# Five cross-partition totals moved inside a slab, four adaLN sums as products with ones, and second-block inputs moved later in a two-layer encoder kernel

## The reference, cut to what matters

```
shift, scale, gate = split(c @ w_ada + b)        # adaLN, once per sub-layer
u = x * (1 + scale) + shift
y = mixer(u)  or  conv_gated_mlp(u)
x = layer_norm(alpha * x + (1 + gate) * y, g, b)

mixer:  a,g,q,k,v = split(u @ w_in)
        h = silu(layer_norm(dwconv31(a * sigmoid(g))))
        o = attention(rotary(q), rotary(k), v)     # window of two 64-token chunks, with sinks
        y = concat(h, o) @ w_out
mlp:    val, gate = split(u @ w_up);  y = (val * silu(dwconv3(gate))) @ w_down
```

## Time and profile before

| what | before |
|---|---|
| time, median of 3 runs | 2124.24 us (2122.6 to 2124.82) |
| the profiled run, its span | 2124.59 us, 2122.7 us |
| TensorE busy | 2076.3 us, 98% |
| weight loads (beside the matmuls) | 1707.1 us, 80% |
| VectorE / ScalarE / GpSimd busy | 56% / 48% / 66% |
| chain that ended last | TensorE 77%, GpSimd 9%, VectorE 5%, ScalarE 4%, issue 3%, DMA 1% |
| mean granted clock of TensorE | 0.992 |
| DMA | 250 MB, mean 118 GB/s |

### The profile page before, as it was taken

One profiled execution on the slowest core, in us unless ns is written; L12 is line 12 of the kernel. 1 busy time (PEld: TensorE's weight loads), 2 busy tenths in 40 slices (PEclk: granted clock), 3 DMA queues, 4 the chain that ended last, 5 costly groups with the idle time before them and its releaser, 6 DMA issues.

```text
span 2122.7 us, 27312 instructions
## 1 busy us (share of the span) xinstructions
PE 2076.3 (98%) x9603; PEld 1707.1 (80%) x9603; DVE 1189.1 (56%) x1949; ACT 1025.4 (48%) x1830; POOL 1404.7 (66%) x1773
## 2 busy tenths in 40 slices
PE   7999999999999999999999999999999999999997
PEld 6877778787888788888788888888778888888887
DVE  5887878676514554777542545587651354332225
ACT  3574357564515665364642656235462465333332
POOL 4986767765767887875557885564546776545554
PEclk9999999999999999999999999999999999999999
DMA  8644544533434354553233333432323333434332
GB/s 296 157 131 137 159 123 137 163 109 100 123 116 124 96 159 139 155 152 99 78 100 100 113 106 92 106 96 74 95 77 104 94 96 90 124 101 123 97 92 77
DMA packets 421508, 250.06 MB, mean 118 GB/s; under 512 B 48149, under 2 KB 393085, under 8 KB 421373
## 3 DMA queue, kind: packets, MB, share of 16 engines
q1 hardware_dynamic: 420506, 248.03, 39.6%
q10 hardware_dynamic: 867, 0.29, 0.1%
HBM read 242.71 MB, written 4.26 MB: 116 GB/s over the span
## 4 chain that ended last, share of the span: by engine, by line
PE 77%; POOL 9%; DVE 5%; ACT 4%; issue 3%; DMA 1%; SPq 1%; POOLq 0%; DVEq 0%; ACTq 0%
PE fg L853 25%; PE fg L855 24%; PE fg L854 24%; POOL w_lo L1856 5%; POOL ada_acc L1927 1%; PE bank_s L939 1%; DVE bank_c L1471 1%; DMA first_ada<-in_w_ada_mix_dram 1%; ACT ada L1262 1%; POOL ssum L1983 1%; PE bank_l L865 1%; PE bank_l L876 1%; ACT w_hi L1112 1%; PE bank_t L948 0%; PE bank_t L961 0%
## 5 line engine op out<-in xcount | busy, mean ns | idle before, releaser
L1856 POOL TENSOR_TENSOR w_lo<-raw,w_hi 128x256 fp32r<-128x256 f32 (+1 forms) x1425 | 1030.1, 754 | 642.1 <-ACT w_hi L1112 641.0
L853 PE MATMUL fg<-u_hi,w_hi 128*128 128x512 f32 x2112 | 841.4, 398 | 5.3 <-POOL w_lo L1856 1.8
L855 PE MATMUL fg<-u_hi,w_lo 128*128 128x512 f32 x2112 | 826.4, 391 | 0.0
L854 PE MATMUL fg<-u_lo,w_hi 128*128 128x512 f32 x2112 | 826.2, 391 | 0.0
L1112 ACT ACTIVATE w_hi<-raw 128x1024 fp32r<-128x1024 f32 (+2 forms) x387 | 375.5, 970 | 390.2 <-PE fg L855 295.9
L853 PEld LDWEIGHTS fg<-u_hi,w_hi 128*128 128x128 f32 x2112 | 398.7, 189 | 103.0 <-issue 15.8
L855 PEld LDWEIGHTS fg<-u_hi,w_lo 128*128 128x128 f32 x2112 | 398.4, 189 | 84.7
L854 PEld LDWEIGHTS fg<-u_lo,w_hi 128*128 128x128 f32 x2112 | 398.8, 189 | 81.9 <-issue 2.9
L1471 DVE SCALAR_TENSOR_TENSOR bank_c<-glu,par,bank_c 128x512 f32<-128x512 f32 x448 | 306.2, 748 | 0.1
L1810 DVE SCALAR_TENSOR_TENSOR x<-fg,mod,x 128x512 f32<-128x512 f32 (+1 forms) x168 | 121.6, 724 | 322.6 <-PE fg L855 322.4
L855 PE MATMUL fg<-h_hi,w_lo 128*128 128x512 f32 (+1 forms) x704 | 270.1, 384 | 0.0
(11 more groups left out here) (253 smaller groups left out, 1849.4 us busy)
## 6 DMA issues: line engine op xcount, KB each, us to landing
raw<-in_w_up_dram SPq DMA_DIRECT2D x176, 512.0 KB, 3.8
ada<-in_w_ada_ffn_dram SPq DMA_DIRECT2D x48, 512.0 KB, 4.6
raw<-in_w_down_dram SPq DMA_DIRECT2D x64, 384.0 KB, 3.5
raw<-in_w_in_dram SPq DMA_DIRECT2D x40, 512.0 KB, 4.0
raw<-in_w_down_dram SPq DMA_DIRECT2D x64, 320.0 KB, 3.1
ada<-in_w_ada_mix_dram SPq DMA_DIRECT2D x32, 512.0 KB, 4.3
raw<-in_w_in_dram SPq DMA_DIRECT2D x32, 256.0 KB, 3.8
raw<-in_w_out_dram SPq DMA_DIRECT2D x32, 256.0 KB, 2.9
```

Source lines behind the costliest of these rows:

```text
L853: pe.matmul(out, hi[:, k, :], rhi, start=k == order[0], stop=False)
L854: pe.matmul(out, hi[:, k, :], rlo, start=False, stop=False)
L855: ins = pe.matmul(out, lo[:, k, :], rhi, start=False, stop=k == order[-1])
L1856: ins = pool.tensor_tensor(lo_of(n)[:, ks, :], raw[n % NRAW][:, ks, :], hi_of(n)[:, ks, :].bitcast(F32), ALU.subtract)
```

## The change

1. `INSIDE` gets five entries more: TensorE does the totals `cm 1`, `cm 3` and the sum `as 12`, `as 18` behind 2 input tiles of the next slab, and `xm 2` behind 4.
2. The sums `as` of chunks 4 to 7 are taken by four products of an `ada_acc` tile with a column of ones (128x1) in place of four transposes; ScalarE copies the 128x4 result to `mod` in place of VectorE's reduction. They no longer charge VectorE's budget, so that taps move up.
3. The steps `iu` and `il` go from slabs 5 to 12 to slabs 5, 6, 7, 10, 11, 12, 13, 13.
4. The Newton rounds of the last pair of token tiles keep their temporary in `bank_s` (PSUM) instead of `small` (SBUF), behind a wait for ScalarE's last read of that bank.

```diff
-INSIDE = {("cm", 0): 2, ("cv", 0): 4, ("xm", 0): 4, ("xr", 0): 6}
+INSIDE = {("cm", 0): 2, ("cv", 0): 4, ("xm", 0): 4, ("xr", 0): 6,
+          ("cm", 1): 2, ("xm", 2): 4, ("cm", 3): 2, ("as", 12): 2, ("as", 18): 2}
...
+ONES_CHUNKS = (4, 5, 6, 7)
...
-        put(ns[-1] + 2, "as", c)
+        if c in ONES_CHUNKS:
+            at(ns[-1] + 2, "as", c)
+        else:
+            put(ns[-1] + 2, "as", c)
...
-    for k in range(DT):
-        put(5 + k, "iu", 1, k)
-        put(5 + k, "il", 1, k)
+    for k, n in enumerate((5, 6, 7, 10, 11, 12, 13, 13)):
+        put(n, "iu", 1, k)
+        put(n, "il", 1, k)
...
+        def copied(c):
+            return (ada_copied, c - CHUNKS_BEFORE + 1) if c in ONES_CHUNKS else (ada_reduced, c - ONES_CHUNKS[-1])
...
-                take(SUM_BANK[c], ada_copied, c - CHUNKS_BEFORE + 1)
+                take(SUM_BANK[c], *copied(c))
-                turned(out, lambda i: ada_acc[c % 2][:, i * P:(i + 1) * P]).then_inc(ada_sum, 1)
+                src = ada_acc[c % 2]
+                if c in ONES_CHUNKS:
+                    for i in range(TB):
+                        ins = pe.matmul(out[:, i:i + 1], src[:, i * P:(i + 1) * P], ones_1[:, 0:1], start=True, stop=True)
+                    ins.then_inc(ada_sum, 1)
+                else:
+                    turned(out, lambda i: src[:, i * P:(i + 1) * P]).then_inc(ada_sum, 1)
...
+            def copy_ada(c):
+                l, ffn, j = c // NCHUNK // 2, c // NCHUNK % 2, c % NCHUNK
+                act.wait_ge(ada_sum, c - CHUNKS_BEFORE + 2)
+                out = bank_t if SUM_BANK[c] == "t" else bank_l
+                act.activation(mod[:, l, ffn, j * TB:(j + 1) * TB], out[:, 0:TB], ACT.Copy).then_inc(ada_copied, 1)
...
+                    elif what == "as" and step[1] in ONES_CHUNKS:
+                        copy_ada(step[1])
...
-                dve.wait_ge(ada_copied, last - CHUNKS_BEFORE + 1)
+                dve.wait_ge(*copied(min(last, ONES_CHUNKS[-1])))
+                if last not in ONES_CHUNKS:
+                    dve.wait_ge(*copied(last))
...
-                dve.tensor_reduce(mod[:, l, ffn, j * TB:(j + 1) * TB], tokens_of(out), AX.X, ALU.add).then_inc(ada_copied, 1)
+                dve.tensor_reduce(mod[:, l, ffn, j * TB:(j + 1) * TB], tokens_of(out), AX.X, ALU.add).then_inc(ada_reduced, 1)
...
+                if pair:
+                    dve.wait_ge(tail_norm, 2)
+                    tt = bank_s[:, 0:2]
...
-                elif what == "as":
+                elif what == "as" and step[1] not in ONES_CHUNKS:
```

More of the change, by code:

```diff
@@ L587, in build @@
         x_t_done, x_evac = sem("x_t_done"), [sem("x_evac0"), sem("x_evac1")]
-        first_add, first_sum, ada_mul, ada_sum, ada_copied = (sem(n) for n in ("first_add", "first_sum", "ada_mul", "ada_sum", "ada_copied"))
+        first_add, first_sum, ada_mul, ada_sum, ada_copied, ada_reduced = (sem(n) for n in ("first_add", "first_sum", "ada_mul", "ada_sum", "ada_copied", "ada_reduced"))
         ada_add = {"pool": sem("ada_add_pool"), "dve": sem("ada_add_dve")}
```

## The result

The changed kernel takes 2107.39 us (median of 4 runs, 2107.15 to 2109.53) against 2123.42 us before on the same chip: ratio 0.9924, 95% interval 0.9912 to 0.9936, so 0.8% faster. The forecast was 2112.3 with a range of 2108.0 to 2117.0: right in direction, 4.9 us too high, and outside its range by 0.6 us. The profiled run took 2107.35 us, its span is 2105.4.

The account below looks back on a forecast made before the run. TensorE, busy in 98% of the span, was taken as the bound. Gains of 14.45 us less 2.5 lost took 11.95 from the profiled 2124.59, giving 2112.6, or 2112.3 against the median of 2124.24; range 2108.0 to 2117.0.

Parts of the forecast that it names:

- cm 0: First total of the first convolution norm: TensorE's 4.07 us wait and the slow clock behind it go, 7.0 us gained.
- Five entries: Five sums moved inside the next slab cover their own waits on TensorE: 6.25 us gained, bounds 5 and 7.
- The end: Last Newton rounds with their temporary in PSUM: 0.6 us gained, between 0.2 and 1.8, some squarings still slow.
- Slab 14: TensorE's new wait there for the second block's later inputs: 0.7 us lost, between 0.3 and 1.5.
- The products: Four adaLN sums by products with ones cost TensorE 1.8 us more, hardly hidden; lower bound 1.3.
- Rival 3: Products with ones cost the rule's price: 3.1 us more, 2115.4; chance 0.02.
- The rotations: Remainder moved from ahead of k's rotation: TensorE gains 0.6 us at the first scores, still waits 2.0.
- the loss at slab 11: Slow clock behind the wait at the first scores, 1.7 to 1.9 us lost, expected to stay.
- The fall in slab 34: Granted clock at 0.51 from 274.4 to 277.9 us, no gain counted; priced at 1.8 us if gone.
- Rival 1: Clock falls at slab 11 and at 274 us both fail to appear, 1.8 us each: 2108.7; chance 0.15.

Follow-up runs that it names:

- e5: Changed kernel with the sums of chunks 4 to 7 again by transposes and VectorE's reduction, taps left at their new places: 2106.91 us, ratio 0.9920.
- e1: Kernel before with only the five new entries of INSIDE: 2116.53 us, ratio 0.9965.
- e3: Kernel before with only the later places of the second block's inputs: 2123.37 us, ratio 0.9999.
- e2: Kernel before with only the four sums of chunks 4 to 7 by products with ones, and the taps this moves up: 2117.29 us, ratio 0.9966.
- e10: Changed kernel with twelve repeats of slab 26's first matmul, delaying TensorE 2.72 us from there: 2109.83 us, ratio 0.9934.
- e9: Changed kernel with six repeats of slab 26's first matmul, delaying TensorE 1.36 us from there: 2109.92 us, ratio 0.9934.
- e14: Changed kernel with six repeats of slab 26's first matmul, the same kernel as e9 run again: 2109.65 us, ratio 0.9936.
- e7: Changed kernel run again with nothing edited: 2106.49 us, ratio 0.9917.
- e13: Kernel before with eight repeats of slab 26's first matmul, delaying all behind it 1.81 us: 2125.92 us, ratio 1.0011.
- e11: Changed kernel with six repeats of slab 2's first matmul, near 52 us: 2109.97 us, ratio 0.9936.

## Why the prediction came out too high

- **`cm 0`, 7.0 us:** right (7.1), by its steps. e5 shows that the taps did it.
- **Five entries, 6.25 us:** right in the trace (6.6), and nothing came back (e1). Low as a value over many runs, since a wait removed can also take a fall with it.
- **The end, 0.6 us:** right, with the slow squarings where they were put.
- **Slab 14, 0.7 us:** 1.0, within its bounds. Alone it would have been 1.6 (e3); the earlier tap was rightly counted.
- **The products, 1.8 us:** the price of one was right (0.81 against 0.85), the sum was not: 0.46 stood in the wait at the first scores, and chunk 7's took VectorE's reduction out of TensorE's way (-0.2 in place of +0.45, e5). "Nothing hides them but perhaps the last" was the failing sentence. Slab 19 gave another 0.6, a wait of the attention for VectorE's `u_lo`, gone also in e2 and e5; it was at nothing in the forecast. Rival 3 set the price of a product by the factor between transposes and products; the row compares products of one column with transposes of 128, so 0.81 us is the price of this product and no test of that factor.
- **The rotations:** this is the step that failed, in two sentences. "So no more than 0.6 of the 1.28 us is gained by TensorE" took the start of k's sums from the earlier trace rows and not their length. The start was right: 0.58 us came from it. 0.47 came from the first sum, 1.05 together (e3, the new places alone: 1.1), chunk 4's products took up to 0.46 more, and of 2.6 us of wait 1.0 was left, not 2.0. The 0.47 could not be counted on: e10, with the same instructions up to there, did not get it and kept 1.6 us of wait. "I keep the loss at slab 11 as it is" then kept a fall that, by 18 profiles, goes with the longer wait: 1.6 us. It was absent at 1.6 and 1.7 us of wait too (e10, e5); at 2.0, the forecast wait, no profile shows what happens.
- **The fall in slab 34, 1.2 us:** kept because it was in the one trace. It is there in half the profiles, with old and new places, and that it was absent in the profile of the changed kernel is in part luck. The Trainium skill (TensorE: Matmul & The Clock Gate, "What's actually happening") was quoted for it, that the same kernel loses differently from run to run, and e9 against e14 agrees. For the first scores it is no guide: there the length of the wait separated 18 profiles.
- The rest (start of the run -0.7, weights in slab 316 -0.6, slabs 28, 32 and 132 +0.95) is small and in the main of the run: in e7, the same kernel, slab 28 takes 0.3 us less than here, slab 132 0.3 less and slab 32 0.2 more.

Rival 1, both falls gone, was the case that happened, at 0.15, and even its 2108.7 is 1.3 us too high. It should have been weighed higher: the forecast held two falls as if they were costs of the kernel. Of the 4.9 us of error 0.8 is not of the change: the forecast was set against a median of 2124.24, and with the fourth run of before it is 2123.42. The profiled run of before (2124.59) lay 1.2 us above that, so that the trace shows 17.2 us and the times 16.0. What brings the fall in slab 34 in one launch and not in another was not settled: it came and stayed away with one and the same kernel (e9, e14), so that e13, one profile, does not show that its delay took it.

## What to carry to other kernels

When a transfer or remainder is moved out from ahead of the engine that releases a wait, read the length of the releasing operation too and not only its start: here 0.5 us of it hung on a near tie between two engines, and a gain of that kind should be given a chance and not a value. Ask of each term that sits on one engine whether it falls into a wait of that engine, and what the other engine did with the time it got. And take a slow stretch behind a short stand from several profiles, or give it half its price: one fell away with its wait, another comes and goes by itself.

## What the runs showed of the hardware

The granted clock fell behind a stand of 2.1 us or more at one place in 8 of 8 profiles, and behind 0 to 1.7 us there in none of 10; behind 2.7 us at another (`xm 2`, with GpSimd's sum as the releaser) in 3 of 6; and behind 2.5 us of thin work ahead of slab 34, where TensorE stood only 0.5 us, in 9 of 18. Each such fall cost 1.2 to 3.0 us, where the waits elsewhere differ by at most 0.4 us between two profiles of the changed kernel (the first and e7, behind the start). One sum of VectorE (64 x 512, all in SBUF) took 1.14 us in all seven profiles in which a piece of GpSimd's work had begun 0.12 to 0.15 us before it. In the eleven in which the two began within 0.03 us of each other it took 0.67 or 0.68 us in nine, and GpSimd's piece then 1.26 to 1.29 us; in e10 and e11 it took 1.27 and 1.25 us and GpSimd's piece 0.72 and 0.74. Which of the two has the long time in such a tie, the start times in the trace do not tell.
